# The router of a mixture of experts, fed from the residual stream before the norm, in a hybrid Hyena and RG-LRU step

## What is computed

```
x = x + g1 * m                                        # m: the mixer's output
h = rms_norm(x, norm_moe[i]) * (1 + sc2) + sh2        # sc2, sh2: per stream (context or latent) and channel
x = x + g2 * moe_ffn(h, router_w, router_bias, w1[i], w3[i], w2[i])

# moe_ffn: group-limited top 2 of 16 experts
scores = softmax(xf @ router_w);  sel = scores + router_bias
best_group = argmax over 4 groups of the sum of the top 2 of sel
idx = top 2 of sel inside best_group;  gates = scores[idx] / sum(scores[idx])
expert e on its tokens: (silu(x @ w1[e]) * (x @ w3[e])) @ w2[e], then weighted by gates and added
```

## Time and profile before

| what | value |
|---|---|
| median of 3 runs | 1558.67 us (1554.54 to 1565.6) |
| the profiled execution | 1558.35 us |
| its span, first to last instruction | 1556.5 us |
| mean granted TensorE clock | 0.994 |
| TensorE busy, products | 1497.0 us (96%) |
| DVE busy, ACT busy | 610.9 us (39%), 316.6 us (20%) |
| moved by DMA | 495.31 MB, 318 GB/s over the span |

### The profile page before, as it was taken

How to read it: one execution, slowest core, us unless ns; L and a number is a source line. 1 busy time by engine, 2 the same in 40 slices (tenths; PEclk the granted TensorE clock), 3 DMA queues, 4 the chain that set the end, 5 groups by cost and what they waited for, 6 DMA issues and landing times.

```text
span 1556.5 us, 21504 instructions
## 1 busy us (share of the span) xinstructions
PE 1497.0 (96%) x7870; PEld 718.3 (46%) x7871; DVE 610.9 (39%) x1815; ACT 316.6 (20%) x535; POOL 0.2 (0%) x4
## 2 busy tenths in 40 slices
PE   9999999999899999989999899999999999999997
PEld 4545555654444344434354355555344434344433
DVE  4535666333324322322333448745122332322233
ACT  4422222131010011011010357623011011111001
POOL 0000000000000000000000000000000000000000
PEclk9999999999999999999999999999999999999999
DMA  9547766762969999999996601535999999999992
GB/s 341 192 159 301 261 251 252 302 280 109 427 273 405 424 426 427 424 428 425 426 422 247 237 1 55 203 122 217 374 423 424 428 426 415 428 426 428 424 395 102
DMA packets 67713, 495.31 MB, mean 318 GB/s; under 512 B 4609, under 2 KB 21265, under 8 KB 28369
## 3 DMA queue, kind: packets, MB, share of 16 engines
q1 hardware_dynamic: 66048, 489.33, 76.9%
q10 hardware_dynamic: 1616, 5.33, 1.1%
HBM read 493.06 MB, written 1.58 MB: 318 GB/s over the span
## 4 chain that ended last, share of the span: by engine, by line
PE 79%; DMA 10%; DVE 6%; ACT 3%; issue 1%; ACTq 0%; DVEq 0%; SPq 0%
PE PS L849 77%; DMA halves<-in_moe_w 10%; PE PS L853 2%; DVE xc L1880 1%; ACT hT L579 1%; DVE halves L1698 0%; DVE misc L1698 0%; DVE halves L1689 0%; DVE halves L1691 0%; ACT hT L832 0%; DVE halves L1517 0%; DVE halves L1690 0%; ACT halves L643 0%; ACT halves L745 0%; ACT h L644 0%
## 5 line engine op out<-in xcount | busy, mean ns | idle before, releaser
L849 PE MATMUL PS<-halves,hT 128*64 128x512 f32 x3072 | 670.7, 595 | 14.5 <-DMA halves<-in_moe_w 12.0
L849 PEld LDWEIGHTS PS<-halves,hT 128*64 128x64 f32 x3072 | 218.2, 137 | 448.6 <-issue 428.2
L849 PE MATMUL PS<-hT,halves 128*128 128x384 f32 x640 | 214.9, 490 | 0.1
L849 PE MATMUL PS<-halves 128*32 128x512 f32 (+5 forms) x928 | 192.6, 502 | 1.8 <-ACT halves L542 0.7
L849 PEld LDWEIGHTS PS<-hT,halves 128*128 128x128 f32 x640 | 119.3, 190 | 98.0 <-issue 18.2
L1960 DVE COPY misc<-PS 64x512 f32<-64x512 f32 x32 | 21.9, 683 | 321.2 <-PE PS L849 321.2
L849 PEld LDWEIGHTS PS<-halves 128*128 128x128 f32 (+2 forms) x928 | 96.3, 157 | 84.0 <-issue 42.7
L1880 DVE SCALAR_TENSOR_TENSOR xc<-PS,MOD,xc 128x128 f32<-128x128 f32 x336 | 112.4, 410 | 13.8 <-PE PS L849 11.8
L849 PE MATMUL PS<-stack,h 128*128 128x128 f32 x768 | 93.6, 280 | 6.0 <-issue 4.9
L849 PEld LDWEIGHTS PS<-stack,h 128*128 128x128 f32 x768 | 89.5, 194 | 18.7 <-issue 17.1
L616 ACT ACTIVATE hT<-PS 128x512 f32<-128x512 f32 x32 | 19.1, 597 | 311.7 <-PE PS L853 311.7
(11 more groups left out here) (240 smaller groups left out, 1031.6 us busy)
## 6 DMA issues: line engine op xcount, KB each, us to landing
halves<-in_moe_w SPq DMA_DIRECT2D x192, 2048.0 KB, 18.2
halves<-in_ada_w SPq DMA_DIRECT2D x48, 1024.0 KB, 6.5
halves<-in_hy_w_in SPq DMA_DIRECT2D x12, 1024.0 KB, 5.1
halves<-in_rg_w_in SPq DMA_DIRECT2D x4, 2048.0 KB, 19.3
halves<-in_hy_w_out SPq DMA_DIRECT2D x4, 1024.0 KB, 9.4
halves<-in_rg_w_out SPq DMA_DIRECT2D x2, 2048.0 KB, 10.2
halves<-in_rg_wa SPq DMA_DIRECT2D x1, 2048.0 KB, 8.5
halves<-in_rg_wx SPq DMA_DIRECT2D x1, 2048.0 KB, 12.6
```

Of the source, the lines that this page charges most:

```text
L849: return nc.tensor.matmul(out, lhsT, rhs, start=start, stop=stop)
```

## The change

1. **The router takes the residual.** DVE scales the router matrix with the modulation once per stream (`rw_mod`), ahead of the residual adds. TensorE multiplies it with `xc` as soon as the sums of squares are issued (`router_raw`), and multiplies the plain router matrix with the shift for a bias. DVE then only scales the raw logits by the reciprocal root. Six small products with a fold matrix (`fold`) add the four column groups and transpose in one; they replace three transposes and the reduction over the groups.
2. **ACT does the modulation there.** All eight tiles of the norm ahead of the experts are modulated by ACT, four before Exp and four behind it; the token tiles follow in the order 0, 2, 4, 1, 3, 5. DVE multiplies six tiles before the maximum and two behind it.
3. **First places at once.** The iota starts at 1, so ranks need no subtraction and no filling with -1; the picks of experts 0 and 1 are two operations straight from the ranks; the gate weights follow the counts.
4. **The spins.** In the norm ahead of the experts all three go, two new ones stand behind the fold products, of eight in the router two remain, and the two of the first expert in the loop go, with the branch around them.

The core of the diff:

```diff
-    put("iota_base", np.tile(np.arange(BASE), (P, 1)))
+    put("iota_base", np.tile(np.arange(BASE) + 1, (P, 1)))
+    put("fold", np.tile(np.eye(32)[:, 0:NE], (4, 1)))
...
 # ACT, after the norm's root
+                act.wait_ge(S("bias_mm"), l + 1)
+                a.activation(bias_col, PS[:, 4, 0:2], ACT.Copy).then_inc(S("bias_ev"), 1)
+                act.wait_ge(S("raw_mm"), l + 1)
+                a.activation(pre[:, 0, :], PS[:, 5, 0:N], ACT.Copy).then_inc(S("raw_ev"), 1)
                 table(ACT.Exp)
-                act.wait_ge(S("rt_mm"), before("rt_mm", l) + 1)
-                a.activation(pre[:, 0, :], PS[:, 0, 0:N], ACT.Copy).then_inc(S("rt_ev"), 1)
-                token_tile(0)
+                modulate(2 * l + 1, range(4))
                 act.wait_ge(S("rt_max"), before("rt_max", l) + 1)
                 a.activation(rt(0), rt(0), ACT.Exp).then_inc(S("rt_exp"), 1)
-                for i in range(1, 6):
-                    token_tile(i)
+                modulate(2 * l + 1, range(4, KD))
+                for n in range(6):
+                    token_tile(n)
...
 # TensorE
             def norm(tag):
                 norm_sums(tag)
-                if tag == 1:
-                    pe.wait_ge(S("v_in"), 16)
-                spin(1, bank=3)
-                norm_spread(tag)
-                spin(2, bank=3)
+                if tag % 2:
+                    router_raw(tag // 2)
+                    norm_spread(tag)
+                else:
+                    spin(1, bank=3)
+                    norm_spread(tag)
+                    spin(2, bank=3)
...
+            def router_raw(l):
+                pe.wait_ge(S("rw_mod"), l + 1)
                 for kk in range(2):
                     for j in range(4):
+                        last = mm(PS[32 * j:32 * j + 32, 4, 0:2], rw[:, j + 4 * kk, :], MOD[:, l, 8 * SH2 + j + 4 * kk, :],
                                   kk == 0, kk == 1)
+                last.then_inc(S("bias_mm"), 1)
+                for s, cs in streams:
+                    for kk in range(2):
+                        for j in range(4):
+                            last = mm(PS[32 * j:32 * j + 32, 5, cs], rw_mod[:, s, j + 4 * kk, :], xc[:, j + 4 * kk, cs],
+                                      kk == 0, kk == 1)
+                last.then_inc(S("raw_mm"), 1)
+
+            def router(l):
+                pe.wait_ge(S("bias_ev"), l + 1)
                 pe.wait_ge(S("rt_ev"), before("rt_ev", l) + 1)
                 for t in range(NT):
-                    last = tr(PS[:, 1, P * t:P * t + P], pre[:, 0, P * t:P * t + P])
+                    s = 0 if t == 0 else 1
+                    out = PS[:, 6, NE * t:NE * t + NE]
+                    mm(out, bias_col[:, s:s + 1].broadcast_to([P, P]), const("fold"), True, False)
+                    last = mm(out, pre[:, 0, P * t:P * t + P], const("fold"), False, True)
                 last.then_inc(S("rt_mm"), 1)
-                for i in range(1, 6):
+                spin(2)
+                for n, i in enumerate(TOKEN_ORDER):
+                    if n in (0, 3):
+                        pe.wait_ge(S("hT_act"), turned_act(2 * l + 1) + 4 * (i % 2) + 4)
                     token_tile(l, i)
-                spin(5)
+                spin(1)
                 pe.wait_ge(S("rt_mask"), before("rt_mask", l) + 1)
...
-                spin(3)
+                spin(1)
                 pe.wait_ge(S("tok"), before("tok", l + 1))
...
                             with pe.If(group > 0):
                                 spread(l, group, done + extra, 0, 4)
-                            with pe.If(group < 1):
-                                passed(done + extra, 0)
-                                spin(2)
...
 # DVE
+                for s in range(2):
+                    ins = v.tensor_tensor(rw_mod[:, s, :, :], rw[:, :, :],
+                                          MODA[:, 2 * l + 1, :, s:s + 1].broadcast_to([P, KD, 32]), ALU.mult)
+                ins.then_inc(S("rw_mod"), 1)
...
+                norm_inverse(tag)
+                dve.wait_ge(S("raw_ev"), l + 1)
+                dve.wait_ge(S("rb_mm"), tag + 1)
+                v.tensor_tensor(pre[:, 0, :], pre[:, 0, :], PS[:, 1, 0:N], ALU.mult).then_inc(S("rt_ev"), 1)
+                norm_apply(tag, range(6))
+                dve.wait_ge(S("rt_mm"), before("rt_mm", l) + 1)
+                logits = PS[:, 6, 0:NT * NE].rearrange("p (t e) -> p t e", t=NT)
+                link(v.tensor_reduce(mx, logits, AX, ALU.max))
+                v.tensor_tensor(L, logits, wide(mx), ALU.subtract).then_inc(S("rt_max"), 1)
+                norm_apply(tag, range(6, KD))
...
-                take(cols[:, 0:3], rankm, 0)
-                take(cols[:, 3:6], gates, 0)
-                link(take(pcols, rankm, 1))
-                for r, column in enumerate((cols[:, 0:3], pcols)):
-                    one_hot(pick[:, :, BASE * r:BASE * r + BASE], base_iota, column, None, BASE, "pick")
+                for r in range(UNROLL):
+                    v.tensor_tensor(pick[:, :, BASE * r:BASE * r + BASE],
+                                    base_iota.unsqueeze(1).broadcast_to([P, NT, BASE]),
+                                    rankm[:, :, r:r + 1].broadcast_to([P, NT, BASE]), ALU.is_equal).then_inc(S("pick"), 1)
                 count_extras(l)
+                gate_weights()
```

More of the change, by code:

```diff
@@ L34 @@
 NX = (N - BASE) // EXTRA
[L37 removed]
+_COLS = [("ident", P), ("earlier_rows", P // 2), ("all_rows", P // 2), ("ones", 32), ("iota_base", BASE), ("iota_extra", EXTRA), ("limits", NX), ("desc", NE), ("fold", NE)]
 _HYENA_COLS = [("fwd_lat", 2 * LAT), ("fwd_ctx", CTX), ("inv_lat", 4 * LAT // 2), ("inv_ctx", CTX)]
@@ L86, in constants @@
     put("ones", np.ones((P, 32)))
-    put("iota_base", np.tile(np.arange(BASE), (P, 1)))
-    put("iota_extra", np.tile(np.arange(EXTRA), (P, 1)))
+    put("iota_base", np.tile(np.arange(BASE) + 1, (P, 1)))
+    put("iota_extra", np.tile(np.arange(EXTRA) + 1, (P, 1)))
+    put("fold", np.tile(np.eye(32)[:, 0:NE], (4, 1)))
     put("desc", np.tile(NE - np.arange(NE), (P, 1)))
@@ L144, in before, with by_act, turned_act, turned_dve @@
     return PER[name] * index
+def by_act(tag):
+    return KD if tag % 2 else BY_ACT
+def turned_act(tag):
+    return sum(by_act(u) for u in range(tag))
+def turned_dve(tag):
+    return KD * tag - turned_act(tag)
 MOE_RELEASE = ("w13_last", "w13_last", "w13_last", "w13_last", "w2_first", "w2_mm")
@@ L575, in modulate @@
                 act.wait_ge(S("modA"), tag + 1)
-                for k in range(BY_ACT):
+                for k in ks:
                     act.wait_ge(S("nrm"), before("nrm", tag) + k + 1)
@@ L591, in norm @@
                 norm_root(tag)
-                modulate(tag)
+                if tag % 2 == 0:
+                    modulate(tag, range(BY_ACT))
             def expert_layer(l):
@@ L684, in mixer0 @@
                 spectrum(1)
-                modulate(0)
+                modulate(0, range(BY_ACT))
                 for ct in range(24):
@@ L1453, in norm_apply @@
                 dve.wait_ge(S("rb_mm"), tag + 1)
-                for k in range(KD):
+                for k in ks:
                     v.tensor_tensor(hT3[:, k, :], xc[:, k, :], PS[:, 1, 0:N], ALU.mult).then_inc(S("nrm"), 1)
             def modulate(tag):
-                l = tag // 2
-                sh = SH2 if tag % 2 else SH1
+                l, sh = tag // 2, SH1
                 dve.wait_ge(S("modA"), tag + 1)
@@ L1469, in norm @@
                 norm_inverse(tag)
-                norm_apply(tag)
+                norm_apply(tag, range(KD))
                 modulate(tag)
@@ L1584, in mixer0 @@
                 halves_joined(0)
-                norm_apply(0)
+                norm_apply(0, range(KD))
                 filter_norm(0)
@@ L1779, in wide @@
                     return ap.unsqueeze(2).broadcast_to([P, NT, n])
-                link(v.memset(chosen[:, 3 * NE:], 0.0))
-                dve.wait_ge(S("rt_mm"), before("rt_mm", l) + 2)
-                parts = PS[:, 1, 0:N].rearrange("p (t j e) -> p t e j", t=NT, j=4)[:, :, 0:NE, :]
-                link(v.tensor_reduce(L, parts, AX, ALU.add))
-                link(v.tensor_reduce(mx, L, AX, ALU.max))
-                v.tensor_tensor(L, L, wide(mx), ALU.subtract).then_inc(S("rt_max"), 1)
+                tag = 2 * l + 1
+                v.memset(chosen[:, 3 * NE:], 0.0)
+                norm_inverse(tag)
[8 more added lines that the diff above has]
+                norm_apply(tag, range(6, KD))
                 dve.wait_ge(S("rt_exp"), before("rt_exp", l) + 1)
@@ L1830, in route, with gate_weights @@
                 mask = e3(chosen[:, 0:3 * NE])
-                link(v.memset(rankm, -1.0))
-                link(v.memset(gates, 0.0))
+                link(v.memset(rankm[:, :, NE:], 0.0))
+                dve.wait_ge(S("rt_mm"), before("rt_mm", l) + 2)
+                ranks = PS[:, 1, 0:NT * NE].rearrange("p (t e) -> p t e", t=NT)
```

(11 more changed lines are left out.)

37 lines of the change are left out of this document (20 added, 17 removed).

## The result

The change made the kernel slower by 5%. The changed kernel takes 1638.02 us (median of 4 runs, 1630.18 to 1642.74) against 1559.58 of the kernel before (4 runs, 1554.54 to 1565.6): ratio 1.0497, 95% interval 1.0468 to 1.0526. The profiled execution took 1641.1 us, its span is 1639.3. The forecast was 1544.6, so 93 us are to be explained.

What follows compares the result with a forecast made beforehand. Bound: the weight stream in late experts, held back by TensorE's slot releases at each layer's head, and DVE and ACT in the routing. 2 x 5.5 + 1.3 + 1.8 = 14.1 us off 1558.35, median 0.3 higher: 1544.6 us, range 1538.5 to 1552.5.

Steps and rivals of the forecast that it cites:

- the sum: Total gain over both layers: 2 x 5.5 + 1.3 + 1.8 = 14.1 us.
- Rival (f): After the routing TensorE stays at 1.2 GHz through gather and first products: slower, 1583.5 us; chance 0.03.
- (a): TensorE's clock falls in the routing wait, costing 1.4 us per layer: 1547.4 us; chance 0.26.
- The bounds behind the range: Bounds of the unknown costs on the total gain, given as 11.6 and 16 us.
- Part 1: Head of the routing: raw products take 1.78 us; Exp, behind ACT's modulation of four tiles, comes 3.5 us earlier.
- Part 2: Places, from mask to gather: 1.4 us instead of 3.4; the gather starts 5.5 us earlier.
- Part 3: First expert's spins removed: 1.3 us saved in layer 0, 1.8 in layer 1 (bounds 0 and 1.8).
- rival (c): First expert in layer 1 gives nothing, a longer low-clock stretch eating its 1.8 us: 1546.4 us; chance 0.07.
- Rival (b): Table load holds ACT twice as long behind the raw products' copy, 1.2 us per layer: 1547.0 us; chance 0.05.
- (d): The weight stream is the bound from further ahead, so the end stays: 1558.7 us; chance 0.05.
- (e): Low-clock stretches vanish and ACT's gaps close: 19.4 us gained, 1539.3 us; chance 0.17.
- The rule weighed: A table change on ACT costs 2.66 us with drain; modulation would start 1.2 us later per layer, sum 11.7.

Runs made afterwards that it cites:

- e5: Changed kernel plus nine unread two-column products on TensorE in layer 0's routing wait: 1546.72 us, ratio 0.9915.
- e8: Changed kernel plus nine unread two-column products in layer 0's routing wait and fifteen in layer 1's: 1550.21 us, a single run.
- e4: Kernel before with only the branch and the first expert's two unread products taken out of the expert loop: 1556.03 us, ratio 0.9975.
- e1: Changed kernel plus nine unread two-column products on TensorE early in the mixer: 1548.44 us, ratio 0.9917.
- e6: Changed kernel plus five unread two-column products (20 instructions) in layer 0's routing wait: 1547.68 us, a single run.
- e12: Changed kernel plus three unread two-column products in layer 0's routing wait: 1648.11 us, ratio 1.0571.
- e2: Kernel before plus thirteen unread two-column products on TensorE early in the mixer: 1633.1 us, ratio 1.0458.
- e3: Changed kernel with the branch and the first expert's two unread products put back into the expert loop: 1637.15 us, ratio 1.0480.
- e9: Changed kernel plus nine unread two-column products in layer 0's routing wait and eighteen in layer 1's: 1635.61 us, ratio 1.0477.
- e10: Kernel before plus eight unread two-column products in the mixer and three inside the expert loop: 1618.41 us, ratio 1.0365.

## Why the prediction was wrong

**The step that failed** is none of the terms of the sum. It is what the whole sum stood on without saying so: that code which the change doesn't touch, the expert loop, runs at its old speed wherever it lies. The working costed each added product by its duration and never as code; 54 instructions ahead of a loop that spanned seven blocks cost 91 us by their place (1638.0 against 1546.7 in e5). No rival held it. Rival (f) had the sign and the wrong mechanism: the clock did fall in the loop, but behind the holes and not out of the routing. In e8, with the same low clock in the routing, it is 1.00 from 440 to 760 us.

The rows of before had the sign already. The wait of 2.60 us at 423.25, which (a) took only for a stretch without work, and the one of 2.13 at 1103.34 are put down to "issue"; both stand in the first pass of a loop, and the queue's packets come there too (7 from 340 to 440 us, none from 440 to 880, 8 from 1060 to 1180). The working asked of neither what TensorE waited for.

**The sum itself held.** With the loop in seven blocks (e5) the change gives 1559.84 - 1546.72 = 13.1 us where 14.1 was forecast, and 0.9915 (0.9891 to 0.9939) where 1544.6 is 0.991. The bounds behind the range don't come out of the working, though: its own terms give 2 x 4.6 + 1.3 + 0 = 10.5 and 2 x 6.0 + 1.3 + 1.8 = 15.1, not 11.6 and 16. The measured 13.1 lies within both.

- **Part 1.** The raw products took about 1.6 us (1.78 forecast), Exp stood behind four modulated tiles 9.0 us after the last add (9.2 forecast).
- **Part 2.** 5.8 us per layer from last add to gather, in both layers (layer 1 of the changed kernel: 16.75), where 5.5 was forecast. The places did as forecast: two comparisons in 0.63 us (0.68), the copies of tokens done at 354.96, just before them.
- **Part 3.** Alone, in e4, 4.0 us by the medians, where 1.3 + 1.8 = 3.1 was forecast; the interval is 0.5 to 7.3 us. In e5 there is no DMA hole behind layer 1's first expert, as forecast; windows of e5 against the earlier trace rows:

```profile
1099.00:1101.00 2.00, 2.00 (x6) 0.50 (x4) 0.00 (x0) 0.00 (x0) 0.00 (x0) 0.50 1.01 426
1111.00:1113.00 2.00, 2.00 (x12) 0.72 (x10) 0.00 (x0) 0.00 (x0) 0.00 (x0) 1.00 1.04 438
1113.00:1115.00 2.00, 2.00 (x12) 0.62 (x10) 0.81 (x2) 0.60 (x1) 0.00 (x0) 1.00 0.99 414
```

The first is the low stretch, which came all the same; the others are at full rate. That agrees with the reading that these holes end when TensorE releases a slot. Whether their 1.8 us reached the end isn't shown: from layer 1's gather to the end e5 takes 474.0 us, e1 472.3 and e6 475.6, against 474.8 before. So rival (c), which gave this term nothing, isn't excluded.

- **Rival (a)** happened and cost nothing: the clock fell to 0.61 and 0.54 at 345 to 349 us of the changed kernel. The fall lies in the two spins behind the fold products (3.34 us for 4 records, 1.96 in e5). The last transposes ended at 353.67, before the mask (354.72). The forecast had the clock at full in the routing; it is in e5's layer 0, but not in its layer 1 (0.65 and 0.50 from 1064 to 1068 us).
- **Rival (b)** is refuted: the load started 0.02 us behind the copy of the raw products (342.62 + 0.49), and ACT was free again 1.5 us after that start.
- **Rivals (d) and (e)**, no gain and 19.4 us, lie outside e5's interval (0.61 to 1.09% of 1559.84, that is 9.5 to 17.0 us). The low stretches of (e) didn't vanish: 0.50 from 1100 to 1102 us of e5.
- **The rule weighed**, the 2.66 us for a change of tables of the Trainium skill (ScalarE: Activation LUTs, "What ACT_TABLE_LOAD costs"): the trace disagrees in the new place too, 1.28 and the dummy's 0.20.

## What to carry to other kernels

An edit also moves all code behind it. Where a long loop's code comes near what the engine's instruction memory holds, look at the instruction queue's packets on the page first: a number that grew by a multiple of the passes, with idle time put down to "issue", means that the loop is fetched again in each pass, and nothing in the edit's own durations explains it. Before an edit is judged by a time, shift the loop by some unread instructions in a wait, and read the packets: here 12 of them made it worse (e12), and 20 (e6) turned a loss of 5% into a gain of 0.8%. A measurement of the kernel as written would have thrown away 13 us that are really there.

## What the hardware showed that was not expected

- **Seven blocks fit and eight don't.** The Trainium skill gives TensorE room for eight blocks of 256 (the section named above). A loop of some 1,560 instructions, two stretches of about 490 of which are mostly skipped, ran without a packet where it lay in seven, and was fetched again whole, 8 to 9 packets a pass, where its end reached some instructions into an eighth. The same section of the Trainium skill also speaks of only two lines, and of a taken branch that waits when its target lies outside a window of two pages. For TensorE the runs show more than two: in seven blocks the jump back to the loop's start cost no packet. Whether one block is always kept for what comes next, or the skipped blocks are fetched too, no run here tells.
- **A fetch behind a jump isn't hidden.** The same section of the Trainium skill says that the cost of crossing a boundary is mostly hidden, and that a taken branch to code that isn't at hand waits for its fetch. In straight code the trace agrees: 12 packets came in the first 340 us of the changed kernel, and TensorE has no wait put down to "issue" there. At the jumps it agrees too: where the loop didn't fit, the holes were mostly 2 to 3 us each (1.0 to 4.1 over all runs), and 6.69 to 8.30 us for two fetches in a row (e12). What it doesn't say is that the first boundary behind such a jump isn't hidden either: 1.0 to 2.9 us at 14 to 20 instructions behind the loop's start (the changed kernel, e2, e3, e9), and 0.78 at most at 40 (e10).
- **The clock pays again.** The holes add up to about 11 us a pass and the pass loses 17: behind the holes products run at a lower granted clock, 0.91 over the pass.
- **It has an edge and no slope.** From 189 to 197, 8 instructions (half a kilobyte, if 256 make the 16.4 KB of a packet), the time fell by 100 us.
